# Both directions of the delta state scan share one level product per chunk, and GpSimd assembles the block matrices from compact inverses

## The reference

```python
    m = jnp.where(strict, jnp.einsum('nbhik,nbhjk->nbhij', kb, kc) * decay, 0.0)
    eye = jnp.eye(CHUNK, dtype=jnp.float32)
    t_inv = lax.linalg.triangular_solve(m + eye, jnp.broadcast_to(eye, m.shape), left_side=True,
                                        lower=True, unit_diagonal=True)
    u = jnp.einsum('nbhij,nbhjv->nbhiv', t_inv, vc * bc[..., None])
    w = jnp.einsum('nbhij,nbhjk->nbhik', t_inv, kb * jnp.exp(gcum)[..., None])
    attn = jnp.einsum('nbhik,nbhjk->nbhij', qc, kc) * decay
...
        v_new = u_i - jnp.einsum('bhck,bhkv->bhcv', w_i, S)
        o = (jnp.einsum('bhck,bhkv->bhcv', q_i * jnp.exp(g_i)[..., None], S)
             + jnp.einsum('bhij,bhjv->bhiv', a_i, v_new))
        g_last = g_i[..., -1:]
        S = (S * jnp.exp(g_last)[..., None]
             + jnp.einsum('bhck,bhcv->bhkv', k_i * jnp.exp(g_last - g_i)[..., None], v_new))
```

## Time and profile before

| | us |
|---|---|
| median of three runs (4647.08 to 4651.04) | 4647.97 |
| the profiled execution, its own time | 4655.05 |
| the profiled execution, its span | 4653.2 |
| stage `delta_scan`, first DMA issue to last output copy | 1493.15 to about 1819 |
| PE busy in the whole span | 4402.6 (95%) |
| DVE, ACT, POOL busy in the whole span | 2805.8, 1819.8, 58.2 |

### The profile page before, as it was taken

One profiled execution on the slowest core, in us unless ns is written; L12 is line 12 of the kernel. 1 busy time (PEld: TensorE's weight loads), 2 busy tenths in 40 slices (PEclk: granted clock), 3 DMA queues, 4 the chain that ended last, 5 costly groups with the idle time before them and its releaser, 6 DMA issues. The chain is left out here.

```text
span 4653.2 us, 76265 instructions
## 1 busy us (share of the span) xinstructions
PE 4402.6 (95%) x29334; PEld 3858.0 (83%) x29334; DVE 2805.8 (60%) x4753; ACT 1819.8 (39%) x2682; POOL 58.2 (1%) x82
## 2 busy tenths in 40 slices
PE   9798999898998996899999999999999999999999
PEld 1594444776998896899999999888888799999999
DVE  0448876575678445654776666555555566775746
ACT  0430000342663332344444555444444455444534
POOL 0000000000000000000000000000000000210000
PEclk9899999988999998999999999999999999999999
DMA  8246555225877331445665555566666445444454
GB/s 328 103 173 252 225 219 205 100 97 191 288 256 222 89 89 37 170 147 198 207 204 193 175 180 176 203 213 213 215 218 215 169 174 175 146 155 154 167 192 158
DMA packets 230390, 848.48 MB, mean 182 GB/s; under 512 B 86465, under 2 KB 124705, under 8 KB 141089
## 3 DMA queue, kind: packets, MB, share of 16 engines
q1 hardware_dynamic: 230176, 845.48, 52.4%
HBM read 794.95 MB, written 50.45 MB: 182 GB/s over the span
## 5 line engine op out<-in xcount | busy, mean ns | idle before, releaser
L283 DVE TENSOR_TENSOR rounded<-arena,rounded 128x1024 fp32r<-128x1024 f32 x320 | 391.8, 1225 | 412.2 <-ACT rounded L276 412.1
L2200 PE MATMUL bank<-rounded,rounded 128*128 128x256 f32 x2048 | 590.7, 288 | 2.7 <-DVE rounded L2325 2.7
L2202 PE MATMUL bank<-rounded,rounded 128*128 128x256 f32 x2048 | 579.9, 283 | 0.0
L2201 PE MATMUL bank<-rounded,rounded 128*128 128x256 f32 x2048 | 579.7, 283 | 0.0
L2955 PE MATMUL bank<-rounded,rounded 128*128 128x256 f32 x1856 | 533.3, 287 | 9.6 <-DVE rounded L3202 5.4
L276 ACT ACTIVATE rounded<-arena 128x1024 fp32r<-128x1024 f32 x320 | 339.0, 1060 | 505.8 <-PE bank L2538 389.2
L2957 PE MATMUL bank<-rounded,rounded 128*128 128x256 f32 x1856 | 525.5, 283 | 0.0
L2956 PE MATMUL bank<-rounded,rounded 128*128 128x256 f32 x1856 | 525.5, 283 | 0.0
L198 PE MATMUL bank<-arena 128*128 128x512 f32 x1024 | 443.2, 594 | 1.3 <-PEq L326 1.3
L3202 DVE TENSOR_TENSOR rounded<-arena,rounded 128x1024 fp32r<-128x1024 f32 x232 | 292.1, 1259 | 240.0 <-ACT rounded L3002 239.5
L2253 ACT ACTIVATE rounded<-arena 128x1024 fp32r<-128x1024 f32 x256 | 271.0, 1059 | 422.4 <-PE bank L2202 421.6
(11 more groups left out here) (450 smaller groups left out, 9639.4 us busy)
## 6 DMA issues: line engine op xcount, KB each, us to landing
arena<-in_w_in SPq DMA_DIRECT2D x244, 1024.0 KB, 4.8
arena<-in_peer_u SPq DMA_DIRECT2D x128, 1024.0 KB, 5.0
arena<-in_peer_v SPq DMA_DIRECT2D x128, 1024.0 KB, 4.8
arena<-in_w_mod SPq DMA_DIRECT2D x96, 1024.0 KB, 6.7
arena<-in_w_out SPq DMA_DIRECT2D x40, 1024.0 KB, 4.8
arena<-in_w_conv_out SPq DMA_DIRECT2D x16, 1024.0 KB, 5.1
arena<-in_w_dn_out SPq DMA_DIRECT2D x16, 1024.0 KB, 4.9
arena<-in_peer_w_q SPq DMA_DIRECT2D x16, 1024.0 KB, 5.6
```

What stands on the lines that cost most here:

```text
L283: dve.tensor_tensor(k.staged(1, q), k.raw(r % 2)[:, c], k.staged(0, q), ALU.subtract).then_inc(k.lo_done, 1)
L2200: pe.matmul(out, wh, hi(kt), start=(kt == 0), stop=False)
L2201: pe.matmul(out, wh, lo(kt), start=False, stop=False)
L2202: mm = pe.matmul(out, wl, hi(kt), start=False, stop=(kt == KT - 1))
```

## The change

In each chunk the two directions' matrices occupy opposite triangles, so one 128 x 128 matrix can hold both where the wanted blocks don't collide: a level is now one product per chunk for both directions (four instead of eight), with operands `n5`, `d5`, `r5`, `n6`, `d6`, `r6` in which some diagonal blocks belong to direction 0 and some to direction 1. The result of a level fills one bank.

- GpSimd makes these operands. Per head it issues 28 copies of 32 partitions each: five groups of four with 4 x 32 elements per partition (`d5`, `n5`, `r5`, `d6`, `r6`) and two groups of four with 256 elements per partition (`invt` and `n6`). It ran two memsets in this stage before.
- The inverses come by two DMAs of 128 x 8 x 32 per head (`plain`, `turned`, one slot each, double buffered) in place of 12. `mat` is now one buffer: `matrix_in(n + 1)` waits until GpSimd has read head n's matrix (`n5_set`, `n6_set`).
- ACT copies the results of `x5_` and `x6_` whole (128 x 512); DVE copies the two corners of `y5_`; both copy the corners of `z5_` and `z6_` (three and one, direction by direction).
- `turn(n)` moves behind `new(h, 1)`, `y5_` behind `old(h, 1)`, `z5_` behind `new(h, 2)`, `x6_` behind `old(h, 2)`. DVE updates the state of step 0 before it scales the keys. `x6_` waits for the scaled keys, where `y5_` did.
- Eight slots (144 to 159) are zeroed by two memsets of GpSimd in `delta_prepare`, before its third `clear`; the gated `y` lies at slot 48 now, and its DMA is issued one head later.

```diff
             for n in range(4):
                 clear(n)
+                if n == 1:
+                    for b in range(2):
+                        pool.wait_ge(m_out[b], 16 * 8)
+                        pool.wait_ge(attn_done, HEADS)
+                    pool.memset(flat(k.t(144, 8)), 0.0)
+                    pool.memset(flat(k.t(152, 8)), 0.0).then_inc(late_zeroed, 1)
...
+    at = lambda slot, n: flat(k.t(slot, n))
+    mat = both(at(16, 4))
+    invt = [both(at(20 + 4 * b, 4)) for b in range(2)]
+    ksc = [both(at(28 + 4 * b, 4)) for b in range(2)]
+    kneg, wt = both(at(36, 4)), both(at(40, 4))
+    plain, turned = ([at(44 + 2 * m + b, 1).rearrange("p (d c t) -> p d c t", d=2, t=32) for b in range(2)] for m in range(2))
+    n5, n6, d5, r5, d6, r6, x5, x6 = (four(at(144 + 2 * m, 2)) for m in range(8))
...
+            def matrix_in(n):
+                if n >= 1:
+                    sp.wait_ge(n5_set, n)
+                    sp.wait_ge(n6_set, n)
+                sp.dma_start(mat.rearrange("p d c t -> p (d c t)"), matrix_of(scratch["m"], n)).then_inc(mat_in, 16)
+
+            def inverses_in(n):
+                if n >= 2:
+                    sp.wait_ge(d6_set, n - 1)
+                    sp.wait_ge(r6_set, n - 1)
+                for m, (dst, done) in enumerate(((turned, turned_in), (plain, plain_in))):
+                    first = 4 * m * P + (n // 8) * 2 * P + (n % 8) * 4
+                    src = bass.AP(scratch["inv"].tensor, first * 1024, [[32, P], [32 * 1024, 8], [1, 32]])
+                    sp.dma_start(dst[n % 2].rearrange("p d c t -> p (d c) t"), src).then_inc(done[n % 2], 16)
...
+            for n in range(1, HEADS):
+                if n + 1 < HEADS:
+                    if n + 1 == 8:
+                        sp.wait_ge(k.inverse_out, 32 * 4)
+                    inverses_in(n + 1)
+                    matrix_in(n + 1)
+                    values_in(n + 1)
...
+        @block.gpsimd
+        def _(pool):
+            def from_diagonal(dst, src, use, done):
                 for b in range(4):
-                    first = 4 * m * P + (h // 8) * 2 * P + (h % 8) * 4 + b
-                    src = bass.AP(scratch["inv"].tensor, first * 1024, [[32, 32], [32 * 1024, 8], [1, 32]])
-                    at = slice(32 * b, 32 * b + 32)
-                    sp.dma_start(dst[at, :, :, at].rearrange("p d c t -> p (d c) t"), src).then_inc(done, 16)
-
...
+                    ins = pool.tensor_copy(dst[quarter(b), :, quarter(b)], src[quarter(b), use[b]])
+                ins.then_inc(done, 1)
+
+            for n in range(HEADS):
+                pool.wait_ge(plain_in[n % 2], 16 * (n // 2 + 1))
+                if n >= 1:
+                    pool.wait_ge(x5_ready, n)
+                from_diagonal(d5, plain[n % 2], (0, 1, 0, 1), d5_set)
+                pool.wait_ge(mat_in, 16 * (n + 1))
+                for d, b, c in ((0, 0, 1), (1, 1, 0), (0, 2, 3), (1, 3, 2)):
+                    ins = pool.tensor_copy(n5[quarter(b), :, quarter(c)], mat[quarter(b), d, :, quarter(c)])
+                ins.then_inc(n5_set, 1)
+                pool.wait_ge(turned_in[n % 2], 16 * (n // 2 + 1))
+                if n >= 1:
+                    pool.wait_ge(y5_ready, n)
+                    pool.wait_ge(z5_ready, n)
+                from_diagonal(r5, turned[n % 2], (1, 0, 1, 0), r5_set)
+                if n < 2:
...
                 else:
...
+                        pool.wait_ge(new_ready[d], 4 * (n - 1))
+                    pool.wait_ge(w_ready, n - 1)
+                for b in range(4):
+                    ins = pool.tensor_copy(invt[n % 2][quarter(b), :, :, quarter(b)], turned[n % 2][quarter(b)])
+                ins.then_inc(invt_set, 1)
+                if n >= 1:
+                    pool.wait_ge(x6_ready, n)
+                for b, d, wide in ((0, 0, HIGH), (1, 0, HIGH), (2, 1, LOW), (3, 1, LOW)):
+                    ins = pool.tensor_copy(n6[quarter(b), :, wide], mat[quarter(b), d, :, wide])
+                ins.then_inc(n6_set, 1)
+                from_diagonal(d6, plain[n % 2], (0, 0, 1, 1), d6_set)
+                if n >= 1:
+                    pool.wait_ge(z6_ready, n)
+                from_diagonal(r6, turned[n % 2], (1, 1, 0, 0), r6_set)
...
+            def level(out, lhs, rhs, ready):
+                for c in range(CHUNKS):
+                    mm = pe.matmul(out[:, c, :], lhs[:, c, :], rhs[:, c, :], start=True, stop=True)
+                mm.then_inc(ready, 1)
+
+            def x5_(n):
+                pe.wait_ge(n5_set, n + 1)
+                pe.wait_ge(d5_set, n + 1)
+                if n >= 1:
+                    pe.wait_ge(x6_kept, n)
+                level(ahead(n, X5), n5, d5, x5_ready)
+
+            def y5_(n):
+                pe.wait_ge(r5_set, n + 1)
+                pe.wait_ge(x5_kept, n + 1)
+                if n >= 1:
+                    pe.wait_ge(w_kept[1], n)
+                level(ahead(n, Y5), r5, x5, y5_ready)
+
+            def z5_(n):
+                level(ahead(n, Z5), x5, r5, z5_ready)
+
+            def x6_(n):
+                pe.wait_ge(n6_set, n + 1)
+                pe.wait_ge(d6_set, n + 1)
+                pe.wait_ge(y5_kept, n + 1)
+                pe.wait_ge(ksc_done, 2 * (n + 1))
+                pe.wait_ge(kneg_done, 2 * (n + 1))
+                level(ahead(n, X6), n6, d6, x6_ready)
...
-                level(sides(h, X5), mat[h % 2], inv5, x5_ready)
-
-            def y5_(h):
-                pe.wait_ge(invt_in[h % 2], 64 * (h // 2 + 1))
-                pe.wait_ge(ksc_done, 2 * (h + 1))
-                pe.wait_ge(kneg_done, 2 * (h + 1))
...
-                    pe.wait_ge(y5_kept[d], h + 1)
-                level(sides(h, X6), mat[h % 2], inv6, x6_ready)
-
-            def z6_(h):
-                for d in range(2):
-                    pe.wait_ge(x6_kept[d], h + 1)
-                    pe.wait_ge(z5_kept[d], h + 1)
-                level(sides(h, Z6), x6, invt[h % 2], z6_ready)
+                    pe.wait_ge(z5_kept[d], n + 1)
+                level(ahead(n, Z6), x6, r6, z6_ready)
 
...
                 after = h + 1 < HEADS
                 new(h, 0)
                 w_(h)
-                if after:
-                    turn(h + 1)
                 old(h, 0)
                 if after:
                     x5_(h + 1)
                 new(h, 1)
                 if after:
-                    y5_(h + 1)
+                    turn(h + 1)
                 old(h, 1)
                 if after:
-                    z5_(h + 1)
+                    y5_(h + 1)
                 new(h, 2)
                 if after:
+                    z5_(h + 1)
+                old(h, 2)
+                if after:
                     x6_(h + 1)
-                old(h, 2)
                 new(h, 3)
                 if after:
                     z6_(h + 1)
                 old(h, 3)
...
+            def x5_out(n):
+                act.wait_ge(x5_ready, n + 1)
+                if n >= 1:
+                    act.wait_ge(z5_ready, n)
+                act.copy(x5, ahead(n, X5)).then_inc(x5_kept, 1)
...
+            def z5_out(n):
+                act.wait_ge(z5_ready, n + 1)
+                act.wait_ge(invt_set, n + 1)
+                act.wait_ge(r6_set, n + 1)
+                z = ahead(n, Z5)
+                for b in (0, 2):
+                    act.copy(invt[n % 2][quarter(b), 0, :, quarter(b + 1)], z[quarter(b), :, quarter(b + 1)])
+                act.copy(r6[quarter(2), :, quarter(3)], z[quarter(2), :, quarter(3)]).then_inc(z5_kept[0], 1)
...
+            def y5_out(n):
+                dve.wait_ge(y5_ready, n + 1)
+                dve.wait_ge(d6_set, n + 1)
+                y = ahead(n, Y5)
+                dve.tensor_copy(d6[quarter(1), :, quarter(0)], y[quarter(1), :, quarter(0)])
+                dve.tensor_copy(d6[quarter(2), :, quarter(3)], y[quarter(2), :, quarter(3)]).then_inc(y5_kept, 1)
+
+            def z5_out(n):
+                dve.wait_ge(z5_ready, n + 1)
+                dve.wait_ge(invt_set, n + 1)
+                dve.wait_ge(r6_set, n + 1)
+                z = ahead(n, Z5)
+                for b in (1, 3):
+                    dve.tensor_copy(invt[n % 2][quarter(b), 1, :, quarter(b - 1)], z[quarter(b), :, quarter(b - 1)])
+                dve.tensor_copy(r6[quarter(1), :, quarter(0)], z[quarter(1), :, quarter(0)]).then_inc(z5_kept[1], 1)
+
+            def z6_out(n):
+                dve.wait_ge(z6_ready, n + 1)
+                dve.tensor_copy(invt[n % 2][HIGH, 1, :, LOW], ahead(n, Z6)[HIGH, :, LOW]).then_inc(z6_kept[1], 1)
...
             for h in range(HEADS):
                 n = h + 1
                 w_kept_(h)
+                new_state(h, 0)
                 if n < HEADS:
                     scaled(n, ksc[n % 2], k.kdec, ksc_done)
...
                 new_state(h, 1)
                 if n < HEADS:
...
+                    y5_out(n)
+                    scaled(n, kneg, k.negegc, kneg_done)
                 new_state(h, 2)
                 if n < HEADS:
```

(67 more changed lines are left out.)

204 lines of the change are left out of this document (77 added, 127 removed).

## The result

| | before | changed |
|---|---|---|
| median (range) | 4649.51 (4647.08 to 4654.1), 4 runs | 4574.82 (4570.76 to 4579.26), 4 runs |
| ratio | | 0.9838, 95% interval 0.9821 to 0.9855 |
| profiled execution, own time | 4655.05 | 4570.76 |
| one pass of the scan | 19.52 | 14.32 |
| first DMA of the stage to the first `new` | 22.3 | 19.9 |

A forecast was written before the change was run, and what follows sets the result against it. PE's records were taken to bound each scan pass; fewer records and changed waits cut it from 19.52 to 14.4 us, 77 us over fifteen passes, giving 4571 us, range 4557 to 4600.

The forecast's parts named there:

- PE's records: In the scan, each of five levels loses eight PE records: 40 x 0.112 = 4.48 us a pass.
- The old wait goes, new ones come: PE's 1.4 us wait before `y5_` goes; waits of 0.3 before `new(h, 1)` and 0.5 before `new(h, 2)` come.
- The pass: One pass of the scan: 19.52 - 4.48 - 1.4 + 0.3 + 0.5 = 14.4 us.
- GpSimd's price: GpSimd's 28 copies take 9.8 us a head, at 0.30 and 0.48 each; memsets give 6.7, two-input arithmetic up to 13.8.
- The slower rival: GpSimd's copies above 0.70 us on average make the kernel slower; at 0.9, 85 us lost, 4733; chance 0.05.
- The matrix: The single-buffered matrix lands 4.8 us after issue; GpSimd waits at `n5` from 19.6 to 21.2; loop 11.5 us, under 14.4.
- The start: Before the first `new`, levels near 4.5 us shorter or more cancel against later arrivals: 0 taken, bounds -3 and +4.
- The whole: Fifteen passes save 77 us: profiled execution 4655.05 to 4578, and the median, 7.1 lower, 4571.

The follow-up runs named there:

- the repeat: The changed kernel again, unaltered, beside two reordered kernels on one chip: 4573.34 us, ratio 0.9836 to the kernel before.
- The half products alone: The kernel before with four products a level instead of eight, direction 1's inverses not computed, copies, DMAs and order kept: 4582.49 us, passes of 15.23 us.
- the matrix late: The changed kernel with the next matrix's DMA held back until GpSimd has made `d5` of that head: 4573.52 us.
- the run past the kernel before: The changed kernel with twenty-four small GpSimd copies and four wide `n6` copies a head also made into spare space: 4668.76 us, ratio 1.0047 to the kernel before.

## Why the prediction was right

Forecast 4571 (range 4557 to 4600), measured 4574.82.

- **PE's records**, 4.48 us a pass: right. The levels have 640 records instead of 1280, and PE's busy time in the fifteen passes is 66.9 us less, 4.46 a pass. Putting them back costs 3.48, and the waits that they then cover (0.30, 0.56, and the slow first records behind them) make up the rest.
- **The old wait goes, new ones come**: right in place and size, 0.3 and 0.5 forecast, 0.30 and 0.56 in the trace. One change of DVE's order removes the larger, so its cause is shown, not argued; the smaller one goes when products that need no state stand ahead of it.
- **The pass**, 14.4 forecast, 14.32 measured: 5.20 x 15 = 78 us.
- **GpSimd's price**: 9.8 us a head forecast, 10.2 measured. The bounds held. The small copy was dearer (0.335, not 0.30), the wide one cheaper (0.44, not 0.48): between 128 and 256 elements a copy grows by 0.83 ns an element, with some 0.23 us fixed. The Trainium skill ("GPSIMD Engine Reference", section 3.1) gives about 1.8 cycles an element as the best case of a tight unrolled loop, 1.5 ns at 1.2 GHz, and 1.03 cycles, 0.86 ns, for short loop bodies that the ports bound; the trace's slope of 0.83 ns agrees with the second. The sum came near because a larger fixed part made up for the smaller slope.
- **The slower rival**: its threshold of 0.70 us a copy is enclosed from both sides. At 0.66 on average the passes are still shorter (18.79 against 19.52), and the whole, 4645.06 in a single run, lies among the times of the kernel before, so no gain of the whole is shown there; 0.71 is a loss of 0.47%. That the sum sets the pass one for one beyond PE's 14.3 holds in the mean of fifteen passes, with single passes far to both sides.
- **The matrix**: it landed 3.5 us after its issue instead of 4.8, and in the passes GpSimd never waited for it, where the paper had a wait of 1.6 us. That wait lay in GpSimd's slack and touched no sum.
- **The start**: 0 taken, -2.4 measured, inside the bounds (-3 to +4); in the repeat -2.1 (20.2 us). The half products alone gave -4.6 (17.7 us in the old order), near the 4.5 forecast, so the rest of the change costs 2.2 there.
- **The whole**: the passes and the start give 80 us, the medians 74.7 and 74.4, both within the intervals. The two profiled executions differ by 84.3, of which 4.9 were gained before the stage's first DMA (1488.25 instead of 1493.15). Nothing shows that as an effect of the change: in the ten kernels that are the same as the changed one up to there the stage began anywhere from 1483.17 to 1496.84, and the two with the old stage before it (1493.15 and 1489.82) lie inside. Scatter of this size would be enough for the 4 to 13 us by which the runs of one kernel lie apart. Whether the 5 us between 80 and 75 are more than that stays open. The passes and the start gained 3 us more than forecast and the medians 2 us less, so part of the nearness of 4571 to 4574.82 is luck.

## What to carry to other kernels

Work taken from the engine that bounds a stage is time until the next wait is uncovered, and which wait that is can be written down beforehand from start-to-start times and the order of each engine's queue; here this found the two waits to 0.1 us, and both could be removed by a reordering. An idle engine may take a pass's small copies if the sum of their start-to-start times stays under the pass: below that sum the passes here did not change (the stage's start did), above it each microsecond counted. Price a repeated instruction over many passes, not in one: one stretched group made three of my expectations wrong.

## What the runs showed of the hardware that was not expected

A DVE instruction with two SBUF inputs holds GpSimd's copies back. DVE's 128 x 1024 product (1.22 us) stretches the group of four copies beside it by 1.00 us (2.71 instead of 1.71), whichever group it is: `n6` in the changed kernel, `n5` with the matrix late (2.29 instead of 1.27), and single small groups where they are doubled (2.2 to 2.3); without the product no group is stretched. A single copy takes nearly all of it: the longest of `n6`'s has 1.39 us, the median 0.40. DVE's other instructions of the pass, which read PSUM and at most one SBUF tile, did nothing of the kind, and DVE's own time stayed 1.22. By the Trainium skill ("SBUF — State Buffer", section "SBUF: two separate sides") DVE and GpSimd share a port pair, and such a DVE instruction and a GpSimd instruction that reads SBUF exclude each other for a whole instruction; the stretch of 1.00 us beside a product of 1.22 agrees.

A PE that waits also lost clock here. With GpSimd's groups doubled the granted clock of the passes is 0.93, and 0.90 in the run past the kernel before; it is 1.00 in the kernel before, where the longest idle time of PE in a pass is 1.25 us. The eight records of `x6_` after an idle time of 3.91 us ran at a granted clock of 0.50, the lower of the two levels (1.2 GHz), and took 2.05 us instead of 1.06:

```profile
1621.28:1623.30 2.02, 2.02 (x9) 2.02 (x10) 1.23 (x5) 0.67 (x3) 1.75 (x7) 0.50 0.18 44
```
